# Twenty-four modulation blocks leave the output projections and are summed inside the latent attentions

## The reference

```python
for l in range(DEPTH):
    mod = (jax.nn.silu(c) @ w_mod[l] + b_mod[l])[:, None, :]
    mod_c = jax.nn.silu(c_ctx) @ w_mod[l] + b_mod[l]
    sh1, sc1, ga1, sh2, sc2, ga2 = jnp.split(mod, 6, axis=-1)
    ...
    h = modulate(rmsnorm(x, g_norm1[l]), sh1, sc1)
    pf, mq, mk, mv, mo, mg, cq, ckv, kr = split_proj(h @ w_in[l])
    y_f = fourier_mix(pf)
    ...
    y_a = merge_heads(blocked_attend(qn, qr, (lat_keys, ctx_keys)))
    x = x + ga1 * (jnp.concatenate([y_f, y_m, y_a], axis=-1) @ w_out[l])
    x = x + ga2 * sqrelu_mlp(modulate(rmsnorm(x, g_norm2[l]), sh2, sc2), w_up[l], w_down[l])
```

## Time and profile before

| | |
|---|---|
| median of 3 runs | 3381.79 us (3380.13 to 3390.01) |
| profiled execution, device time | 3395.01 us |
| profiled execution, span on the core | 3392.9 us |
| PE busy | 3129.4 us (92%) |
| DVE busy | 1759.7 us (52%) |
| ACT busy | 1159.2 us (34%) |
| POOL busy | 302.4 us (9%) |
| DMA | 280.28 MB, mean 83 GB/s |
| mean granted TensorE clock | 0.961 |

### The profile page before, as it was taken

One profiled execution on the slowest core, in us unless ns is written; L12 is line 12 of the kernel. 1 busy time (PEld: TensorE's weight loads), 2 busy tenths in 40 slices (PEclk: granted clock), 3 DMA queues, 4 the chain that ended last, 5 costly groups with the idle time before them and its releaser, 6 DMA issues. The chain is left out here.

```text
span 3392.9 us, 47639 instructions
## 1 busy us (share of the span) xinstructions
PE 3129.4 (92%) x18472; PEld 2702.8 (80%) x18472; DVE 1759.7 (52%) x2667; ACT 1159.2 (34%) x1810; POOL 302.4 (9%) x268
## 2 busy tenths in 40 slices
PE   3999887999997899889999998999999999899997
PEld 2678776888886687768887897899999898778885
DVE  8538686454545547663333435554344335554443
ACT  3343633222222344533344332243223332243222
POOL 0000210101102000102223000010001000010001
PEclk8999898999998999789999999999999999999998
DMA  6201042333322111222222111122222111122322
GB/s 259 66 18 61 7 161 91 108 111 111 112 99 102 41 40 44 88 81 96 96 93 94 51 44 44 50 87 82 104 88 99 70 38 51 56 88 88 108 87 89
DMA packets 102380, 280.28 MB, mean 83 GB/s; under 512 B 35904, under 2 KB 36032, under 8 KB 100832
## 3 DMA queue, kind: packets, MB, share of 16 engines
q1 hardware_dynamic: 97568, 262.39, 22.1%
q0 software_dynamic: 3808, 10.38, 1.0%
q10 hardware_dynamic: 864, 5.57, 0.4%
HBM read 276.17 MB, written 2.10 MB: 82 GB/s over the span
## 5 line engine op out<-in xcount | busy, mean ns | idle before, releaser
L340 PE MATMUL ps<-h_hi,hi_ring 128*128 128x512 f32 (+1 forms) x2416 | 828.7, 343 | 90.9 <-DVE h_lo L657 62.5
L259 ACT ACTIVATE hi_ring<-ring 128x1024 fp32r<-128x1024 f32 (+1 forms) x410 | 419.8, 1024 | 1125.2 <-PE ps L340 1085.3
L340 PE MATMUL ps<-h_lo,hi_ring 128*128 128x512 f32 (+1 forms) x2416 | 799.4, 331 | 0.0
L340 PE MATMUL ps<-h_hi,lo_ring 128*128 128x512 f32 (+1 forms) x2416 | 796.6, 330 | 0.0
L269 DVE TENSOR_TENSOR lo_ring<-ring,hi_ring 128x1024 fp32r<-128x1024 f32 (+1 forms) x410 | 487.4, 1189 | 575.7 <-ACT hi_ring L259 571.6
L340 PEld LDWEIGHTS ps<-h_hi,hi_ring 128*128 128x128 f32 x2416 | 463.2, 192 | 167.3 <-issue 101.7
L340 PEld LDWEIGHTS ps<-h_lo,hi_ring 128*128 128x128 f32 x2416 | 464.5, 192 | 44.9 <-issue 3.3
L340 PEld LDWEIGHTS ps<-h_hi,lo_ring 128*128 128x128 f32 x2416 | 462.3, 191 | 41.8
L340 PE MATMUL ps<-ffn_operand,hi_ring 128*128 128x264 f32 (+1 forms) x2112 | 479.7, 322 | 1.5 <-DVE lo_ring L269 1.5
L340 PEld LDWEIGHTS ps<-ffn_operand,hi_ring 128*128 128x128 f32 x2112 | 350.7, 188 | 35.1 <-issue 1.8
L340 PE MATMUL ps<-ffn_operand,lo_ring 128*128 128x264 f32 (+1 forms) x1056 | 339.1, 321 | 0.0
(11 more groups left out here) (347 smaller groups left out, 3847.8 us busy)
## 6 DMA issues: line engine op xcount, KB each, us to landing
ring<-weights_dram SPq DMA_DIRECT2D x334, 512.0 KB, 3.2
mod_ring<-w_mod_dram SPq DMA_DIRECT2D x64, 512.0 KB, 4.2
ring<-weights_dram SPq DMA_DIRECT2D x76, 384.0 KB, 2.8
arena<-w_mod_dram SPq DMA_DIRECT2D x32, 512.0 KB, 3.9
x<-x_dram SPq DMA_DIRECT2D x1, 3072.0 KB, 16.9
arena<-c_rows_dram ACTq DMA_DIRECT2D x3, 1024.0 KB, 6.4
arena<-ret_decay_dram POOLq DMA_DIRECT2D x2, 1056.0 KB, 6.1
silu_rows<-c_rows_dram ACTq DMA_DIRECT2D x2, 1024.0 KB, 5.3
```

What stands on the lines that cost most here:

```text
L259: self.nc.scalar.activation(self.hi_ring[:, g % SPLIT, 0:w], self.ring[:, g % RING, 0:w], ACT.Copy).then_inc(self.hi, 1)
L340: ins = nc.tensor.matmul(out[0:m, c:c + n], w, a[:, t0:t0 + n], start=first and k == 0 and p == 0, stop=last and k == kts - 1 and p == 2)
```

## The change

The sums of blocks 24 to 39 (layer 0) and of the last eight blocks (layer 1) move from `out_projection` into `latent_attention` of the same layer, in a new class `SumsInPlace`. It has no ring: it has two slots, one for c and one for c_ctx, and **each block is loaded twice, once into each slot**. The product is written over the slot itself, so a slot is loaded again only after its own sum. The rows of silu stay where `fourier` made them, in the part of `mix` that the attention writes last; `fourier` of layer 1 now makes them too, as it had no modulation before. The output projections are called without modulation.

```diff
+class SumsInPlace:
...
+    def load(self, sp, first, stop):
+        core = self.core
+        for i in range(first, stop):
+            for c in range(2):
+                if i:
+                    sp.wait_ge(self.made.sem, self.made.at(2 * (i - 1) + c + 1))
+                sp.dma_start(self.slots[:, c, :], core.dram["w_mod"][self.l * MOD_BLOCKS + self.first + i]).then_inc(self.landed[c].sem, 16)
+
+    def sums(self, dve, n):
+
+        core = self.core
+        for at in range(self.given, min(self.given + n, 2 * self.count)):
+            i, c = divmod(at, 2)
+            dve.wait_ge(self.landed[c].sem, self.landed[c].at(16 * (i + 1)))
+            slot = self.slots[:, c, :]
+            core.nc.vector.scalar_tensor_tensor(slot, slot, 1.0, self.rows[:, c, :], ALU.mult, ALU.mult,
+                                                accum_out=core.mod_sum[:, self.first + i, c:c + 1]
+                                                ).then_inc(self.made.sem, 1)
+            self.given = at + 1
...
@@ fourier, ACT and DVE
-            if mods:
-                mod.load_rows(act)
+            mod.load_rows(act)
             norm.on_act(act)
...
+            if not mods:
+                mod.sigmoid(act)
             for j in range(2):
                 act.wait_ge(token.sem, token.at(j + 1))
...
+            if not mods:
+                mod.begin(dve)
...
@@ latent_attention, SP
-            core.feed(sp, LATENT_BLOCKS)
+            if mods:
+                core.feed(sp, 2)
+                mod.load(sp, 0, 1)
+                core.feed(sp, LATENT_BLOCKS - 2)
+                mod.load(sp, 1, mods)
+            else:
+                core.feed(sp, LATENT_BLOCKS)
...
@@ latent_attention, ACT, ahead of the copies into mix
+            if mods:
+                act.wait_ge(mod.made.sem, mod.made.at(2 * mods))
...
@@ latent_attention, DVE
             for j in range(LATENT_BLOCKS - 1):
                 core.part_lo(dve, 0, j + SPLIT)
+                if mods and j == 0:
+                    mod.sums(dve, 2)
...
                 if u + 1 < len(units):
                     peak_of(u + 1)
+                if mods:
+                    mod.sums(dve, 2 + -(-(2 * mods - 2) * (u + 1) // (len(units) - 3)) - mod.given)
                 if u:
                     finish(u - 1)
                 dve.wait_ge(expd.sem, expd.at(u + 1))
                 step(nc.vector.reciprocal(inv[:, u:u + 1], total[:, u:u + 1]))
             finish(len(units) - 1)
+            if mods:
+                mod.finish(dve)
...
@@ build
-                    mod = Modulation(core, l, first, count, free[:, 0:MOD_RING * BLOCK],
-                                     free[:, MOD_RING * BLOCK:].rearrange("p (r n) -> p r n", r=4))
-                    out_projection(core, h, mix, tokens, lambda j, c: core.mod[:, 2, j, c:c + 1], some, tmp, mod)
+                    out_projection(core, h, mix, tokens, lambda j, c: core.mod[:, 2, j, c:c + 1], some, tmp)
```

More of the change, by code:

```diff
@@ L68 @@
 MOD_FOURIER = KT
+MOD_LATE = MOD_FIRST + MOD_FOURIER
 FOURIER_BLOCKS, LATENT_BLOCKS = 2, 4
@@ L171, in __init__ @@
         self.added = self.counter("squares_added")
-        self.mod_used = 0
+        self.mod_used, self.mod_elsewhere = 0, 0
         self.names = 0
@@ L416, in load @@
         sp.dma_start(self.ring[:, g % MOD_RING, :],
-                     core.dram["w_mod"][t * inner + g]).then_inc(core.mod_landed[g % MOD_RING], 16)
+                     core.dram["w_mod"][t * inner + (g + core.mod_elsewhere)]).then_inc(core.mod_landed[g % MOD_RING], 16)
     def feed(self, sp, n=None):
@@ L493, in close, with __init__, finish @@
         self.steps.close(self.n)
+class SumsInPlace:
+    def __init__(self, core, l, first, count, rows, slots):
+        self.l = l
+        self.core, self.first, self.count, self.rows, self.slots = core, first, count, rows, slots
+        self.landed = [core.counter(f"late_mod_landed_{c}") for c in range(2)]
+        self.made = core.counter("late_mod_sum_done")
+        self.steps, self.n = core.counter("mod_steps"), 0
+        self.given = 0
+    def load(self, sp, first, stop):
[15 more added lines that the diff above has]
+            self.given = at + 1
+    def finish(self, dve):
+        core, v = self.core, self.core.nc.vector
+        self.sums(dve, 2 * self.count)
+        dve.wait_ge(self.made.sem, self.made.at(2 * self.count))
+        step = Steps(dve, self.steps)
+        b0, b1 = self.first, self.first + self.count
+        at = P_BMOD + self.l * MOD_BLOCKS
+        b = core.param[:, at + b0:at + b1]
+        mod = core.mod[:].rearrange("p s k c -> p (s k) c")[:, b0:b1, :]
+        step(v.tensor_tensor(mod, core.mod_sum[:, b0:b1, :], b[:, :, None].to_broadcast([P, b1 - b0, 2]), ALU.add))
+        if b0 <= 4 * KT < b1:
+            gn = core.param[:, P_G2 + self.l * KT:P_G2 + (self.l + 1) * KT]
+            step(v.scalar_tensor_tensor(core.gain[:, 1, :, :], core.mod[:, 4, :, :], 1.0,
+                                        gn[:, :, None].to_broadcast([P, KT, 2]), ALU.add, ALU.mult))
+        self.n = step.n
+    def close(self):
+        for s in self.landed:
+            s.close(16 * self.count)
+        self.made.close(2 * self.count)
+        self.steps.close(self.n)
+        self.core.mod_elsewhere += self.count
@@ L941, in fourier @@
     sin = [a(LT, half[0]), a(CT, half[1])]
-    mod = Modulation(core, l, mod_first, mods, mix[:, 2:KT, :].rearrange("p k n -> p (k n)")[:, 0:MOD_RING * BLOCK],
-                     a(4, BLOCK)) if mods else None
+    mod = Modulation(core, l, mod_first, mods, a(MOD_RING, BLOCK).rearrange("p r n -> p (r n)"),
+                     silu_rows(mix))
     norm.tmp = a(2, ALL)
@@ L1037, in fourier @@
     core.close(FOURIER_BLOCKS, FOURIER_BLOCKS)
-    if mods:
-        mod.close()
+    mod.close()
     norm.close()
@@ L1045, in fourier, with silu_rows, latent_attention @@
     odd_in.close(0 if mods else 2)
-def latent_attention(core, arena, acts, l, mix, ctx_queries):
+def silu_rows(mix):
+    return mix[:, 2:KT, :].rearrange("p k n -> p (k n)")[:, 0:4 * D].rearrange("p (r n) -> p r n", r=4)
+def latent_attention(core, arena, acts, l, mix, ctx_queries, mod_first=0, mods=0):
     nc, dram = core.nc, core.dram
@@ L1078, in latent_attention @@
     pair_rows = lambda h: slice(h % 2 * A_NOPE, (h % 2 + 1) * A_NOPE)
+    mod = SumsInPlace(core, l, mod_first, mods, silu_rows(mix)[:, 0:2, :], silu_rows(mix)[:, 2:4, :]) if mods else None
     tables = core.counter("tables_in")
@@ L3043, in build @@
                     fourier(core, arena, acts, mix, tokens, norm, l, MOD_FIRST, 0 if l else MOD_FOURIER)
-                    latent_attention(core, arena, acts, l, mix, not last)
+                    first, stop = ((MOD_LATE, MOD_BLOCKS - KT), (MOD_BLOCKS - KT, MOD_BLOCKS))[l]
+                    latent_attention(core, arena, acts, l, mix, not last, first, stop - first)
                     m = Mlstm(arena, mix)
@@ L3052, in build @@
                     tmp = arena[:, KT * ALL:(KT + 2) * ALL].rearrange("p (a n) -> p a n", a=2)
-                    free = arena[:, (KT + 2) * ALL:(KT + 2) * ALL + (MOD_RING + 4) * BLOCK]
-                    first, count = ((MOD_FIRST + MOD_FOURIER, MOD_BLOCKS - MOD_FIRST - MOD_FOURIER - KT),
-                                    (MOD_BLOCKS - KT, KT))[l]
-                    mod = Modulation(core, l, first, count, free[:, 0:MOD_RING * BLOCK],
-                                     free[:, MOD_RING * BLOCK:].rearrange("p (r n) -> p r n", r=4))
-                    out_projection(core, h, mix, tokens, lambda j, c: core.mod[:, 2, j, c:c + 1], some, tmp, mod)
+                    out_projection(core, h, mix, tokens, lambda j, c: core.mod[:, 2, j, c:c + 1], some, tmp)
             with parts(ALL) as (h, acts):
```

## The result

| | before | after |
|---|---|---|
| median, us (14 runs each) | 3385.07 (3380.13 to 3391.38) | 3393.30 (3387.40 to 3406.47) |
| ratio | | 1.0024, 95% interval 1.0016 to 1.0033 |
| profiled execution, us | 3395.01 | 3387.53 |
| its span and granted clock | 3392.9, 0.961 | 3385.7, 0.958 |

The median rose by 8.2 us, which is under 0.3%; 3385 was predicted. So the two traces can't be compared by their totals: I compare the same instruction in both, stage by stage.

The account below looks back on a forecast made before the run. DVE was taken to bound the ends of the output projections, PE the attention loop. Terms -11.7 + 12.4 + 2 gave +2.7 on a 3381.8 us median, about 3385 us; range 3374 to 3399.

Parts of the forecast that it names:

- the two large terms: Output projections 11.7 us shorter in both layers together; layer 0's attention loop 12.4 us longer through waits for loads.
- Output projections, -11.7: Without sums, PE starts the next stage earlier: 9.1 us gained in layer 0 and 2.6 in layer 1.
- The start of the next stage: After the output projection ends, the barrier was to take 0.6 us before PE starts the next stage.
- Fourier and head of layer 1, 0: Layer 1's added rows, sigmoid, product and table load hide in fourier; head sums cost nothing, or 1 to 2 us.
- Sums as work, 0: In the attention loops, DVE's added sums fit: a long unit needs 3.1 of 3.26 us in layer 0, 2.6 in layer 1.
- the main case: Chance 0.63: loads land in 3.1 to 3.7 us, loop +10 to +17, net 0 to +8, 3381 to 3390 us.
- the hiding rival: Chance 0.14: landing below 3 us, only DVE's work counts, 5.6 us in layer 0's short units; net -6, 3376 us.
- Loads, +12.4 on the loop: Layer 0's attention loop: load waits set 4.8 us per pair, 12.4 us longer, some 5 in long units, rest in short.
- Clock, +2: PE's low clock at the attention's end and the next stage's head, 1 to 3 us, taken as 2.
- Landing of 3.3 us, fixed: Each load in the attention loop lands in 3.3 us, with a pair's two loads issued 1.15 us apart.
- loads collide: Chance 0.17: loads land in 4.3 us, a pair takes 5.65 us, loop 26 us longer; net +14 to +17, 3397 us.
- The clock falls in the long units (0.06): Chance 0.06: PE's clock drops to 0.50 in layer 0's long attention units, up to 46 us more, 3431 us.

Follow-up runs that it names:

- slots loaded once: Changed kernel with each of the two slots loaded once per layer, so later sums wait for no load and modulation numbers are wrong; 3379.88 us, 0.9980 to before.
- layer 0 alone: Changed kernel with only layer 0's 16 blocks moved into its attention, layer 1 left as in the kernel before; 3399.33 us, 1.0033 to before.
- all sums in long units: Changed kernel with all 30 sums of layer 0's attention loop in its 16 long units, none in the short ones; 3397.75 us, 1.0026 to before.
- half: Changed kernel, but layer 0 makes 8 blocks in the attention's long units and 8 in its output projection, one per weight block; 3377.72 us, 0.9966 to before.
- early: As half, but the output projection's 8 blocks are made in its first six weight blocks; 3373.30 us, 0.9961 to before; repeat 3378.45 us, 0.9967.

## Why the prediction came out as it did

The verdict was right: within 0.3%, above zero, by the two large terms that I named. The sum was 5.5 us too low: the change is +5.4 to +11.2 us by its interval, and my +2.7 lies outside it. A further 3.3 us between 3385 and 3393 is the base, 3381.8 from three runs and 3385.07 from 14. The prediction held that less than 0.3% can't be told from no change; 14 runs of each told 0.24%.

- **Output projections, -11.7.** Right: 12.2 by the ratio of the run without sums, 9.0 and 2.5 by the gaps in PE's time. The wait of 0.63 us was won as well, though PE takes 69.9 us from the first to the last matmul of layer 0's in both traces (429.46 to 499.35, 445.04 to 514.96). Around the wait the splits of the weights are 9.57 us apart in before (448.13 to 457.70) and 8.40 in after (464.66 to 473.06). What cancels it is the stage's head, which takes 19.6 us in after (445.04 to 464.66) and 18.7 in before (429.46 to 448.13). Its first 2.6 us have a lower granted clock in after; first before, then after:

```profile
429.40:432.00 2.60, 2.54 (x9) 2.25 (x10) 2.60 (x4) 2.60 (x5) 0.00 (x0) 0.67 0.99 413
```
```profile
445.00:447.60 2.60, 2.56 (x8) 2.20 (x9) 2.60 (x4) 2.60 (x5) 0.00 (x0) 0.50 0.90 362
```

- **The start of the next stage.** POOL's end releases PE in 0.05 us (521.18 to 521.23), not in the 0.6 I took from the barrier.
- **Fourier and head of layer 1, 0.** Right; both table loads are there (1.28 us each) and both are covered.
- **Sums as work, 0.** Right for the long units. For the short ones the main case had no such term apart from the loads, since I took loads to be slower; the hiding rival put 5.6 us on it. The run with slots loaded once shows 3.1 us there, and 5.9 with what is added behind the loop.
- **Loads, +12.4 on the loop.** Right in cause: 12.1 us in this trace, and 3.1 when the loads don't matter, so 9.0 are theirs. That 12.4 meets 12.1 is partly luck. In layer 0 alone the same loop loses 9.5 us, and the split was wrong. I put 5 us into the long units, which doesn't follow from my own numbers: 4.8 us per pair at 1.44 sums per unit is 3.45 us per unit, 3 us more over 16. They lost 1.9 by unit 15, since a pair turns in 4.5 to 4.9 us there (177.65 to 182.16 above) while the units ask for one in 4.5. The short units lost 10.2 us and not 7.4; the last three loads are late there (next point but one). The idle time per pair is about 1 us and not 2 to 2.5, because the units' own work on DVE lies inside the turn; I had counted the turn less the sums and forgotten that work.
- **Clock, +2.** The mis-sized term. 4.4 us are added behind the loop in the profiled execution of after, 1.0 in that of layer 0 alone, 2.8 with slots loaded once. It is a cost that depends on the execution, and I had its lower part.
- **Landing of 3.3 us, fixed.** Also too simple. In after the 21 loads up to 222 have a median of 3.3, but the last three of the loop 3.9 to 4.3, and in the run with all sums in long units the landing is 4.2 from the sixth load on. So the rival "loads collide" was in part real in its landing times, for some loads of some executions; that transfers collide there is not shown. I also had the two loads of a pair 1.15 us apart. In after only the loop's first two are, and most others come 2.0 to 2.7 us apart, the nearer of my two cases. The terms seen in after's trace add up to +5.3 (12.1 + 4.4 - 8.7 - 2.5), 2.6 above my sum; the 2.9 us from there to the median's +8.2 stand in no trace, since only the profiled execution of each kernel can be looked into. Three executions point to the landing: the fastest of layer 0 alone has 3.1 to 3.5 us to the end, the second fastest of after has three late loads, and the slowest of the long-unit runs has 4.2 nearly throughout. That this is what parts the executions is not shown.
- **The clock falls in the long units (0.06).** Refuted for the changed kernel: 1.00 over its long units, where PE was busy 48.06 of 49.10 us. In the run with all sums there it held 1.00 over 25 us in which PE was busy 73%, and fell later (0.65 from 228 to 236). The section that I weighed (the Trainium skill, "TensorE: Matmul & The Clock Gate", HAM oscillation) tells of matmuls that take less time than the DMA wait behind them; there the clock falls at every wait. I read it too widely, for no wait in the long units was as long as their work. No run here shows that case. In the short units of after the clock fell behind a wait of 2.80 us that follows 3.7 us of work (224.69 to 228.38), and in "half" it fell with no wait of PE above 0.5 us ahead of it.

## What to carry to other kernels

A slot that is refilled only after its own use gives one use per landing and slot; count uses per turn, not bytes alone. Here one load served two sums once a scratch tile took the products, and with that 0.24% lost became 0.24% won. Work moved under an engine that is the bound is free only in units that have room for it, so fill by the room in each unit (the 16 long ones first), leave the rest where it was, and keep it away from the last two blocks of its stage, whose end the next stage waits for (2.1 us by the traces; the medians don't tell it).

## What was not expected of the hardware

- Loads of the same size landed in 3.2 us in one execution and 4.2 in another, and passed from one to the other in the middle of a loop, staying there. No other load of the kernel was under way. A load issued 1.1 us behind another, the second of each loop, landed in 4.0 to 4.2 us in three traces (after, layer 0 alone, all in long units).
- The granted clock from 232 to 245 was 1.00, 0.87, 0.74, 0.61, 0.56 and 0.50 (means) in runs whose short units lie there, and PE was busy 9.8 to 10.7 us of the 13 in all of them (a busy time at the low clock holds less work). Before and "half" have the same PE work from 232 to 236 (3.01 us of 4, at 1.00), and no sum in the short units; from 236 to 240 the clock is 1.00 in one and 0.59 in the other.
- Layer 1's mLSTM stage, which the change doesn't touch, takes 80.6 us between two weight splits in before (1339.30 to 1419.90) and 75.4 in after (1339.91 to 1415.34), with a granted clock of 0.57 and 0.74 in the same 40 us. It makes a good part of the differences between single executions: it takes 83.0 us in "half" and 74.1 in the repeat of "early", 8.9 of the 11.0 us between these two executions. It alone can hide a change of 0.2%. Why it differs is open.

```profile
1340.00:1380.00 40.00, 34.33 (x198) 32.33 (x197) 17.73 (x47) 12.04 (x39) 10.81 (x10) 0.57 0.00 1
```
```profile
1340.00:1380.00 40.00, 34.00 (x250) 31.72 (x251) 22.34 (x65) 17.97 (x61) 11.63 (x11) 0.74 0.00 1
```
